# Start of a two-layer decoder step: early weight loads, a smaller bias scratch, one-hots on 128 partitions

## What is computed

```python
for l in range(DEPTH):
    x = x + 0.5 * swiglu(rmsnorm(x, norm_ffn1[l]), gate1[l], up1[l], down1[l])
    z = rmsnorm(x, norm_mix[l]) @ w_in[l]            # conv | pool | q k v | index q, k, w
    x = x + concat(conv(z), pool(z), sparse_attn(z, caches, rel_bias)) @ w_o[l]
    x = x + 0.5 * swiglu(rmsnorm(x, norm_ffn2[l]), gate2[l], up2[l], down2[l])
y = rmsnorm(x, norm_final)
# inside sparse_attn, for the chosen keys:
logits = q @ k * HEAD_DIM ** -0.5 + rel_bias[bucket(qpos - kpos)]
```

## Time and profile before

| | us |
|---|---|
| median of 3 runs | 2670.68 (2670.45 to 2673.86) |
| the profiled execution | 2664.64 |
| its span, first to last instruction | 2662.8 |
| first weight product starts at | 83.54 |
| TensorE products busy | 2440.0 (92% of the span) |
| VectorE, ScalarE, GpSimd busy | 928.0, 747.7, 930.0 |
| moved by DMA | 264.58 MB, 99 GB/s over the span |

### The profile page before, as it was taken

The page is one execution under the profiler, slowest core; times in us unless marked ns, Lnnn a source line. Parts: engine busy times, 40 slices in busy tenths (PEclk is TensorE's granted clock), DMA queues, the critical chain, the costliest instruction groups (busy, mean ns, idle before and its releaser), DMA issues.

```text
span 2662.8 us, 52553 instructions
## 1 busy us (share of the span) xinstructions
PE 2440.0 (92%) x19371; PEld 2280.4 (86%) x19371; DVE 928.0 (35%) x1652; ACT 747.7 (28%) x1072; POOL 930.0 (35%) x483
## 2 busy tenths in 40 slices
PE   4799999899968899999989999989997879999997
PEld 2799999869835789999989999986984568999996
DVE  2122222398424222222242222246953332222223
ACT  1322222443223332222232222234222333222213
POOL 0533434317400343434433443341650032444331
PEclk6899999899979889999989999999998898999998
DMA  4423332213475222223313333221346731332221
GB/s 89 111 85 93 98 92 86 68 32 96 164 242 187 80 65 87 87 87 95 95 52 103 102 94 89 83 67 34 93 141 205 253 91 48 95 95 79 78 89 47
DMA packets 333955, 264.58 MB, mean 99 GB/s; under 512 B 34962, under 2 KB 283280, under 8 KB 333808
## 3 DMA queue, kind: packets, MB, share of 16 engines
q1 hardware_dynamic: 332792, 260.27, 32.1%
q10 hardware_dynamic: 1032, 2.62, 0.9%
HBM read 253.12 MB, written 9.89 MB: 99 GB/s over the span
## 4 chain that ended last, share of the span: by engine, by line
PE 86%; DVE 3%; SPq 3%; DMA 3%; issue 3%; ACT 2%; DVEq 0%; ACTq 0%; POOLq 0%
PE ps L1233 75%; PE ps L1490 2%; DMA raw<-in_ffn_gate 2%; PE ps L1587 1%; SPq L438 1%; SPq L433 1%; PE ps L1415 1%; PE ps L1511 1%; PE ps L1577 1%; DVE work_p L1080 1%; PE ps L1337 1%; PE ps L1568 0%; PE ps L1401 0%; PE ps L1542 0%; PE ps L1502 0%
## 5 line engine op out<-in xcount | busy, mean ns | idle before, releaser
L813 POOL TENSOR_TENSOR w_lo<-raw,w_hi 128x1024 fp32r<-128x1024 f32 (+1 forms) x336 | 797.2, 2386 | 1300.3 <-ACT w_hi L583 1296.8
L1233 PE MATMUL ps<-h_hi,w_hi 128*128 128x272 f32 x3904 | 813.6, 290 | 62.2 <-DVE h_lo L985 57.1
L1233 PE MATMUL ps<-h_hi,w_lo 128*128 128x272 f32 x3904 | 808.7, 289 | 0.0
L1233 PE MATMUL ps<-h_lo,w_hi 128*128 128x272 f32 x3648 | 754.3, 289 | 0.0
L1233 PEld LDWEIGHTS ps<-h_hi,w_hi 128*128 128x128 f32 x3904 | 614.5, 190 | 65.1 <-DVE h_lo L985 57.9
L1233 PEld LDWEIGHTS ps<-h_hi,w_lo 128*128 128x128 f32 x3904 | 614.1, 190 | 0.0
L1233 PEld LDWEIGHTS ps<-h_lo,w_hi 128*128 128x128 f32 x3648 | 575.7, 190 | 0.0
L583 ACT ACTIVATE w_hi<-raw 128x1024 fp32r<-128x1024 f32 (+1 forms) x336 | 343.6, 1045 | 253.7 <-DMA raw<-in_ffn_gate 213.0
L999 DVE TENSOR_TENSOR gated<-ps,silu 128x544 f32<-128x544 f32 x88 | 63.8, 725 | 912.0 <-PE ps L1233 912.0
L1011 DVE SCALAR_TENSOR_TENSOR xT<-ps,xT 128x544 f32<-128x544 f32 x352 | 255.1, 725 | 265.4 <-PE ps L1233 262.9
L1233 PE MATMUL ps<-act_hi,w_hi 128*128 128x272 f32 x1408 | 292.1, 289 | 9.5 <-DVE act_lo L1004 9.5
(11 more groups left out here) (205 smaller groups left out, 1736.6 us busy)
## 6 DMA issues: line engine op xcount, KB each, us to landing
raw<-in_ffn_gate SPq DMA_DIRECT2D x88, 512.0 KB, 3.8
raw<-in_ffn_up SPq DMA_DIRECT2D x88, 512.0 KB, 4.0
raw<-in_ffn_down SPq DMA_DIRECT2D x88, 512.0 KB, 3.4
ring<-in_cache_k SPq DMA_DIRECT2D x128, 256.0 KB, 4.2
ring<-in_cache_v SPq DMA_DIRECT2D x128, 256.0 KB, 3.7
raw<-in_w_in SPq DMA_DIRECT2D x48, 512.0 KB, 3.8
raw<-in_w_o SPq DMA_DIRECT2D x16, 512.0 KB, 4.0
kipages<-in_cache_kidx SPq DMA_DIRECT2D x128, 32.0 KB, 1.8
```

What stands on the lines that cost most here:

```text
L813: pool.tensor_tensor(w_lo[:, c % 6, 0:n], raw[:, c % 3, 0:n], w_hi[:, c % 6, 0:n].bitcast(F32), ALU.subtract).then_inc(units_split, 1)
L1233: ins = pe.matmul(out[:, hf, :], w, x[:, HT * hf:HT * (hf + 1)], start=first and w is w0 and x is xh, stop=last and w is w1)
```

## The change

`ROWS = 23` rows of scratch are written per head instead of 128. The strip is read with eight transfers of 16 partitions and all heads each, instead of eight of 128 partitions and one head: transfer u covers partitions 16u to 16u+15, from scratch rows u to u+15, its columns shifted by 16u, so that partition p reads the same values as before.

GpSimd opens the three weight slots ahead of its wait for the start instead of behind it.

The one-hots of the sampled tokens are loaded four times, shifted, onto four groups of 32 partitions, and so is the relative bias; with `relx` on 128 partitions, each column block is one product over 128 partitions instead of four over 32. The one-hots of the prompt are a fifth load. Four copies fill `relx` instead of 16.

```diff
--- before.py
+++ after.py
@@ -61,6 +61,7 @@
     _n += _w
 NCONST = _n
 NTD, NTP = LS + DT - 1, SEQ + P - 1
+ROWS = 7 + 16
 
 
 def shape_constants():
@@ -143,7 +144,7 @@
 TOPK_STEPS = 16 * 6 + 32 * 2
 POOL_CHAIN = 43
 OUT_SMALL = 10
-S_IN = 3 + 5 * DEPTH
+S_IN = DT + 2 + 5 * DEPTH
 
 
 def trunk(nc, a):
@@ -201,7 +202,7 @@
         ring = [at(f"ring{n}", [P, 4, WA], r) for n, r in enumerate(
             (r_whi, r_wlo, r_whi + 16384, r_wlo + 16384, r_whi + 8192, r_wlo + 8192))]
         kn_stage = at("kn_stage", [P, 4, WA], r_wlo + 8192)
-        oh = at("oh", [32, NTD + NTP], r_whi)
+        oh = at("oh", [P, LS + NTP], r_whi)
         r_qk, r_q, r_cz = region(4 * TOK * 4), region(4 * TOK * 4), region(4 * TOK * 4)
         qi = at("qi", [P, 4, TOK], r_qk)
         kT = at("kT", [P, 4, TOK], r_qk)
@@ -245,8 +246,8 @@
         stat = at("stat", [P, 2, 8], region(64))
         sstat = at("sstat", [P, 2, 6], region(48))
         ident_b, mask_b[0] = at("ident_b", [P, P], region(256), BF16), at("mask0", [P, P], region(256), BF16)
-        rel_sb = at("rel_sb", [32, NH], region(32))
-        relx = at("relx", [32, DT, P], r_wlo + 4096)
+        rel_sb = at("rel_sb", [P, NH], region(32))
+        relx = at("relx", [P, P], r_wlo + 4096)
         epsb = at("epsb", [P, 1], region(32))
         pt_sb = at("pt_sb", [1, DB * NPG], region(DB * NPG * 4), I32)
         vrows = at("vrows", [P, P], r_wlo + 8192)
@@ -403,7 +404,8 @@
             sp.dma_start(cst[:, :], a['consts']).then_inc(s_cst, 16)
             x_rows(0)
             x_rows(1)
-            sp.dma_start(rel_sb[:, :], a['rel_bias']).then_inc(s_in, 16)
+            for t in range(DT):
+                sp.dma_start(rel_sb[32 * t:32 * t + 32, :], a['rel_bias']).then_inc(s_in, 16)
             sp.dma_start(pt_sb[0:1, :], a['page_table'].rearrange("(o b) n -> o (b n)", o=1)).then_inc(s_in, 16)
             for l in range(DEPTH):
                 for n, v in enumerate(('norm_ffn1', 'norm_mix', 'norm_ffn2')):
@@ -415,7 +417,9 @@
                              a['pool_scale'][l, :].rearrange("(c p) -> c p", p=P)).then_inc(s_in, 16)
             sp.dma_start(vrows[DEPTH * 32:DEPTH * 32 + 8, :],
                          a['norm_final'].rearrange("(c p) -> c p", p=P)).then_inc(s_in, 16)
-            sp.dma_start(oh[:, :], a['onehots']).then_inc(s_oh, 16)
+            for t in range(DT):
+                sp.dma_start(oh[32 * t:32 * t + 32, 0:LS], a['onehots'][:, DT - 1 - t:DT - 1 - t + LS]).then_inc(s_oh, 16)
+            sp.dma_start(oh[0:32, LS:LS + NTP], a['onehots'][:, NTD:NTD + NTP]).then_inc(s_oh, 16)
             for t in range(2, 5):
                 x_rows(t)
 
@@ -509,9 +513,9 @@
                     k_chunk(0, i)
 
                 hold(sp, "sp", s_scr, 16)
-                for h in range(NH):
-                    src = bass.AP(a['scratch'].tensor, h * P * NTP + P - 1, [[NTP - 1, P], [1, SEQ]])
-                    sp.dma_start(strip[:, h, :], src).then_inc(strip_loaded, 16)
+                for u in range(8):
+                    src = bass.AP(a['scratch'].tensor, u * (NTP - 16) + P - 1, [[NTP - 1, 16], [P * NTP, NH], [1, SEQ]])
+                    sp.dma_start(strip[16 * u:16 * u + 16, :, :], src).then_inc(strip_loaded, 16)
 
                 for i in range(HALF):
                     if i < 6:
@@ -653,7 +657,7 @@
             act.activation(tp_sb[:, 0:512], ps[0:NH, 4, :], ACT.Copy, scale=1 / SCALE).then_inc(tp_done, 1)
             act.activation(tp_sb[:, 512:NTP], ps[0:NH, 5, 0:NTP - 512], ACT.Copy, scale=1 / SCALE).then_inc(tp_done, 1)
             act.wait_ge(tp_done, 2)
-            act.dma_start(a['scratch'], tp_sb[:, :].unsqueeze(1).to_broadcast([NH, P, NTP])).then_inc(s_scr, 16)
+            act.dma_start(a['scratch'][:, 0:ROWS, :], tp_sb[:, :].unsqueeze(1).to_broadcast([NH, ROWS, NTP])).then_inc(s_scr, 16)
             act.wait_ge(zeroed, 4)
             act.wait_ge(tiles, T_START)
 
@@ -831,8 +835,8 @@
                     lo(l, ph, 0, c)
 
             pool.memset(pw[:, :, :], 0.0).then_inc(zeroed, 1)
+            pool.sem_inc(units_split, RAW_SLOTS)
             pool.wait_ge(tiles, T_START)
-            pool.sem_inc(units_split, RAW_SLOTS)
 
             with pool.Fori(0, DEPTH) as l:
                 ffn(l, 0)
@@ -1024,12 +1028,13 @@
 
 
             dve.memset(epsb[:, :], EPS).then_inc(zeroed, 1)
-            dve.memset(relx[:, :, :], 0.0).then_inc(relx_done, 1)
+            dve.memset(relx[:, :], 0.0).then_inc(relx_done, 1)
             dve.wait_ge(s_in, 16 * S_IN)
             dve.wait_ge(relx_done, 1)
             for t in range(DT):
-                for b in range(4):
-                    dve.tensor_copy(relx[:, t, :].rearrange("p (b h t) -> p b h t", b=4, h=NH)[:, b, :, t], rel_sb[:, :]).then_inc(relx_done, 1)
+                r = slice(32 * t, 32 * t + 32)
+                dve.tensor_copy(relx[r, :].rearrange("p (b h t) -> p b h t", b=4, h=NH)[:, :, :, t],
+                                rel_sb[r, :].unsqueeze(1).to_broadcast([32, 4, NH])).then_inc(relx_done, 1)
             for t in range(5):
                 dve.wait_ge(tiles, t + 1)
                 r = rows_of(t)
@@ -1325,16 +1330,15 @@
             pe.wait_ge(s_in, 16 * S_IN)
             pe.wait_ge(x_updates, 2)
             pe.transpose(ps[:, 2, 0:nv], vrows[0:nv, :], ident[0:nv, 0:nv]).then_inc(tiles, 1)
-            pe.wait_ge(s_oh, 16)
+            pe.wait_ge(s_oh, 16 * (DT + 1))
             pe.wait_ge(x_updates, 3)
-            pe.matmul(ps[0:NH, 4, :], rel_sb[:, :], oh[:, NTD:NTD + 512], start=True, stop=True)
-            pe.matmul(ps[0:NH, 5, 0:NTP - 512], rel_sb[:, :], oh[:, NTD + 512:NTD + NTP], start=True, stop=True).then_inc(tiles, 1)
+            pe.matmul(ps[0:NH, 4, :], rel_sb[0:32, :], oh[0:32, LS:LS + 512], start=True, stop=True)
+            pe.matmul(ps[0:NH, 5, 0:NTP - 512], rel_sb[0:32, :], oh[0:32, LS + 512:LS + NTP], start=True, stop=True).then_inc(tiles, 1)
             pe.wait_ge(x_updates, 5)
             pe.wait_ge(zeroed, 3)
-            pe.wait_ge(relx_done, 1 + 4 * DT)
+            pe.wait_ge(relx_done, 1 + DT)
             for b in range(3):
-                for t in range(DT):
-                    ins = pe.matmul(ps[:, b, 0:LT], relx[:, t, :], oh[:, DT - 1 - t + LT * b:DT - 1 - t + LT * (b + 1)], start=t == 0, stop=t == DT - 1)
+                ins = pe.matmul(ps[:, b, 0:LT], relx[:, :], oh[:, LT * b:LT * (b + 1)], start=True, stop=True)
             ins.then_inc(tiles, 1)
 
             pe.wait_ge(zeroed, 4)
```

## The result

| | before | changed (lowest to highest run) | ratio (95%) |
|---|---|---|---|
| first series | 2671.01 | 2625.81 (2625.60 to 2633.15) | 0.9835 (0.9817 to 0.9854) |
| second series, beside three of the experiments | 2667.99 | 2632.18 (2630.12 to 2638.39) | 0.9867 (0.9845 to 0.9890) |

Forecast were 2628 and a range of 2619 to 2640. The profiled execution of the changed kernel takes 2625.86, span 2624.0; a second one took 2638.39. Within a series, single runs of the changed kernel lie 7.6 and 8.3 us apart, those of the kernel before 3.4 and 16.1. The two profiles of the changed kernel differ by 12.6 us in span: 6.6 of them lie in the two attention stages, the other 6 in the stages ahead of each.

What follows compares the result with a forecast made beforehand. The kernel was taken to be paced by its products, except for a 46.66 us wait for weights behind the scratch write. 45.9 saved at the start less 3.5 for strips gives 42.4; 2670.68 - 42.4 = 2628, range 2619 to 2640.

Steps and rivals of the forecast that it cites:

- What blocks the start: At the start, the 2.62 MB scratch write at 53 GB/s holds back the weights, a single wait of 46.66 us.
- Steps 1 to 5: Start of the kernel, from the shorter scratch write to the first weight product: 45.9 us saved, first product near 37.6.
- Extra loads: Seven more transfers at the start delay the x rows by 1.7 to 3.5 us; 2.7 taken.
- Bias copy: With one-hot products cut from 12 to 3, it waits for the squares, starting at 26.8 for 31.60; 4.8 us saved.
- GpSimd last of all: Before the first product, GpSimd's low halves end last, up to 41.75; products at 42.4 for 83.54, 41.1 us saved.
- Step 6: Strip loads of 16 partitions in the attention layers: no gain, 0 to 7 us lost for both layers, 3.5 taken.
- My own sign of being wrong: The strips forecast is wrong if the attention stages grow by more than 3.5 us each.
- my slow end: Slowest rate assumed for the strip loads: 106 GB/s, 19.8 us for 2.10 MB.
- the term after it: SyncE's stall issuing value pages behind the strips in a filled queue: 0 to 3.5 us a layer.
- B: Rival: strips are slow and nothing covers them, 14.6 us a layer, 29 in all, time 2654; chance 0.07.
- C: Rival: weight loads go only when one-hot products end; first product at 45, 7.6 us lost, time 2636; chance 0.07.
- D: Rival: slower than before; strips drain at 26 GB/s, some 62 us a layer, 124 lost, time 2749; chance 0.06.

## Why the prediction was right, and where it was not

**What blocks the start: right.** The wait for weights was the scratch write; 39.7 us go with it alone, and 22.2 us with the early slots alone, up to the fourth unit.

**Steps 1 to 5: right.** Forecast was a first product near 37.6; the profiles of the two executions show 38.02 and 37.54. Extra loads: 2.7 us taken, 2.57 (x rows at 10.19 for 7.62) to 3.0 (sample rows at 16.72 for 13.69) seen. (One slip: 0.40 MB at half of 402 GB/s are 2.0 us and not 1.8; the bounds hardly move.) Bias copy: 26.8 forecast, 27.45 seen, behind the squares and not the products. GpSimd last of all, then the low half of h: as worked out. TensorE's slow beginning stayed too: its first pairs of products take 0.65 us until 3.2 us after the first, then 0.41, as before (3.3 us); the granted clock there is 0.50 in the second profile (30 to 41 us), while the clock column of the first, 1.00, does not fit its own product times.

**Step 6, the strips: mechanism right, size wrong.** I bounded the cost of both layers by 0 and 7 us and took 3.5. My own sign of being wrong was a growth of more than 3.5 us in each attention stage, and on average that came. By the experiment that has the strips alone it is 12.4 (7.7 to 17.9). By the profiles: 14 attention stages with neighbours issued by SyncE average 246.2 us (242.1 to 250.3), six at full rate 241.1 (238.5 to 243.0), so about 5 a layer and 10 in all, with a wide spread. The rate itself was better than my slow end (about 140 GB/s against 106); what failed is the term after it. In the 14 stages SyncE stalled by 1.7 to 5.8 us, 3.8 on average (its 16 issues took 16.45 to 20.29 us in place of 14.49 and 14.77), where I had 0 to 3.5 and took the middle. Counted in the traces, the issues there that take 1.1 us or more begin with 12 to 15 transfers not yet landed, mostly 13 or 14; my estimate had 15 and 16 of them outstanding. And I had no term for the clock: at 0.50 the last value products of the first profile took 3.7 us more.

The rule of the Trainium skill ("SBUF — State Buffer", section "Door 1: The DMA port swizzle") was the better guide at this step. By its formula, worked out here as an estimate, 16 neighbours reach four ports, 16 partitions eight apart eight, 32 four apart all sixteen. The order of the rates here, 142, 211 and 339 GB/s, agrees with it; their size is not in proportion, as the two doublings of the ports brought factors of 1.5 and 1.6, the second with loads that land about as fast as they are issued. Its 104 GB/s for the first is below what the runs show; eight such loads stood in a row here, and which of them overlapped is not shown.

**The sum.** With 10 in place of 3.5 the same steps give 45.9 - 10 = 36 us, which is the second series (35.8); the first (45.2) is above it, though the profiled executions of the two kernels differ by 38.8 only. That 2628 lies 2.2 us from the first series is thus in part chance: the spread of the attention stages, some 8 us a layer, is larger than the 6.5 us by which the term was wrong. The traces show what goes with that spread: in the 14 stages TensorE was at 0.50 for 54.6 to 78.5 us, in the six at full rate for 47.8 to 58.0, and the longer stages of the 14 are those with more of it (correlation 0.88). Why one execution has more of it than another stays open, and so does how much of it is cause and how much is the effect of longer waits.

**The rivals.** B, all of the slow strips exposed: a third of its 29 us came by the profiles, two fifths by the experiment. C, weights not early: the kernel with late slots shows its mechanism, 5.5 us for the 7.6 worked out. D did not come: the strips got some 140 GB/s where it had 26 and needed less than 52.

## What to carry to other kernels

A wait for a load need not be the fault of that load: look for what else the engines carried at that time, how many partitions it touched, and how many bytes it could do without. A small transfer's partitions are worth choosing: here 16 of them drained 1.5 times as fast lying eight apart as side by side, and 32 lying four apart 2.4 times as fast as 16 side by side. And where two chains end at nearly the same time, an edit to either alone measures as nothing, so they have to be undone one by one from the finished kernel to see what each is worth.

## What I had not expected of the hardware

Issue is not free of what the engines do: one issue for a value page, 0.34 us in the median, took 4.11 us while the strips drained, and slow transfers on ScalarE's queue made outputs on SyncE's queue land in 13.44 us in place of 2.05. The rate of a load from HBM to 16 partitions differs by half with where they lie (142 and 211 GB/s), and eight partitions read for the scratch write gave 53.
